# High half first: reordering the three products of each weight unit in a two-block transformer on one Trainium2 core

## What is computed

```python
xn = rms_norm(h, g_mix[l]); proj = xn @ w_in[l]          # four mixers on the parts of proj
h = h + jnp.concatenate([ya, yb, yc, yd], axis=-1) @ w_out[l]
h = h + memory_cross_attention(rms_norm(h, g_xa[l]), rms_norm(mem, g_mem[l]), w_xq[l], w_xkv[l], w_xo[l])
h = h + conv_ffn(rms_norm(h, g_ffn[l]), w_up[l], w_ffconv[l], w_down[l])
...
x = x + gmlp_mixer(rms_norm_2(x, a_norm[l]), a_w_in[l], a_v_norm[l], a_w_sp[l], a_b_sp[l], a_w_out[l])
x = x + diff_attention(rms_norm_2(x, b_norm[j]), k, v, b_w_q[j], b_lambda[j], b_subln[j], b_w_o[j], _lambda_init(l))
x = x + swiglu(rms_norm_2(x, ffn_norm[l]), ffn_w_gu[l], ffn_w_down[l])
return rms_norm_2(x, final_norm)
```

## Time and profile before

| | |
|---|---|
| time of the program, median of 3 runs | 2095.79 us (2094.93 to 2101.04) |
| span of the profiled execution | 2093.4 us |
| the median over that span | 2.4 us |
| PE busy, share of the span | 1982.2 us, 95% |
| DVE, ACT, POOL busy | 51%, 39%, 12% |
| mean granted clock of PE | 0.960 of full speed |

### The profile page before, as it was taken

One profiled execution on the slowest core, in us unless ns is written; L12 is line 12 of the kernel. 1 busy time (PEld: TensorE's weight loads), 2 busy tenths in 40 slices (PEclk: granted clock), 3 DMA queues, 4 the chain that ended last, 5 costly groups with the idle time before them and its releaser, 6 DMA issues.

```text
span 2093.4 us, 25748 instructions
## 1 busy us (share of the span) xinstructions
PE 1982.2 (95%) x8818; PEld 1587.6 (76%) x8818; DVE 1073.7 (51%) x1531; ACT 820.3 (39%) x1216; POOL 256.1 (12%) x206
## 2 busy tenths in 40 slices
PE   6988999889999999899999999999998889999998
PEld 5867776766888878788678888877776568888886
DVE  6666546627777732647444443244676454444323
ACT  4235434415554521453344443134454334444212
POOL 3702102002000000400200000010553020000000
PEclk9988889989999999998999999999997799999999
DMA  4321222112222232221222223222211022232322
GB/s 154 101 91 41 71 72 80 61 45 77 100 90 93 97 110 90 72 93 59 80 94 96 95 95 101 90 83 97 71 51 41 11 71 100 100 100 90 100 90 81
DMA packets 48356, 174.37 MB, mean 83 GB/s; under 512 B 5416, under 2 KB 5544, under 8 KB 48048
## 3 DMA queue, kind: packets, MB, share of 16 engines
q1 hardware_dynamic: 46944, 169.50, 24.1%
q10 hardware_dynamic: 1024, 2.94, 0.4%
q0 software_dynamic: 336, 1.25, 0.2%
HBM read 171.57 MB, written 2.10 MB: 83 GB/s over the span
## 4 chain that ended last, share of the span: by engine, by line
PE 77%; DVE 10%; ACT 5%; issue 5%; POOL 3%; DVEq 0%; ACTq 0%; DMA 0%; POOLq 0%; SPq 0%
PE ps L379 25%; PE ps L380 24%; PE ps L381 24%; POOL square_sum L2028 3%; ACT w_hi L870 2%; DVE w_lo L1367 1%; DVE conv_g L1751 1%; DVE conv_a L1751 1%; PE ps L772 1%; DVE xg_lo L1373 1%; DVE x L1414 1%; DVE r_cols L1380 1%; PE ps L783 1%; PE ps L834 1%; PE ps L532 1%
## 5 line engine op out<-in xcount | busy, mean ns | idle before, releaser
L1367 DVE TENSOR_TENSOR w_lo<-w_raw,w_hi 128x1024 fp32r<-128x1024 f32 x302 | 385.6, 1277 | 593.5 <-ACT w_hi L870 593.4
L379 PE MATMUL ps<-xg_hi,w_hi 128*128 128x512 f32 (+2 forms) x1512 | 593.7, 393 | 43.6 <-DVE xg_lo L1373 18.8
L381 PE MATMUL ps<-xg_hi,w_lo 128*128 128x512 f32 (+2 forms) x1512 | 584.8, 387 | 0.0
L380 PE MATMUL ps<-xg_lo,w_hi 128*128 128x512 f32 (+2 forms) x1512 | 584.7, 387 | 0.0
L870 ACT ACTIVATE w_hi<-w_raw 128x1024 fp32r<-128x1024 f32 x302 | 318.0, 1054 | 678.4 <-PE ps L381 678.4
L379 PEld LDWEIGHTS ps<-xg_hi,w_hi 128*128 128x128 f32 x1512 | 286.0, 189 | 129.4 <-DVE xg_lo L1373 30.5
L381 PEld LDWEIGHTS ps<-xg_hi,w_lo 128*128 128x128 f32 x1512 | 286.2, 189 | 57.7
L380 PEld LDWEIGHTS ps<-xg_lo,w_hi 128*128 128x128 f32 x1512 | 286.4, 189 | 54.0
L379 PE MATMUL ps<-hid_hi,w_hi 128*128 (+1 forms) x528 | 210.2, 398 | 3.5 <-DVE w_lo L1367 3.5
L380 PE MATMUL ps<-hid_lo,w_hi 128*128 (+1 forms) x528 | 209.8, 397 | 0.0
L381 PE MATMUL ps<-hid_hi,w_lo 128*128 (+1 forms) x528 | 209.8, 397 | 0.0
(11 more groups left out here) (319 smaller groups left out, 2586.4 us busy)
## 6 DMA issues: line engine op xcount, KB each, us to landing
w_raw<-in_weights SPq DMA_DIRECT2D x315, 512.0 KB, 3.2
x<-in_x_cols SPq DMA_DIRECT2D x2, 1024.0 KB, 6.9
out_cols<-result SPq DMA_DIRECT2D x8, 256.0 KB, 2.2
squares<-in_mem_cols ACTq DMA_DIRECT2D x1, 512.0 KB, 3.7
sp_w<-in_spatial ACTq DMA_DIRECT2D x1, 512.0 KB, 3.5
sp_b<-in_spatial_bias ACTq DMA_DIRECT2D x1, 512.0 KB, 5.2
dil<-in_dil_table POOLq DMA_DIRECT2D x1, 448.0 KB, 6.6
alibi<-in_alibi_table ACTq DMA_DIRECT2D x1, 448.0 KB
```

Source lines behind the costliest of these rows:

```text
L379: nc.tensor.matmul(to, wh, xh, start=start, stop=False)
L380: nc.tensor.matmul(to, wh, xl, start=False, stop=False)
L381: return nc.tensor.matmul(to, wl, xh, start=False, stop=stop)
L1367: nc.vector.tensor_tensor(w_lo[:, u % 2, :], w_raw[:, u % 2, :], w_hi[:, u % 2, :].bitcast(F32), ALU.subtract).then_inc(w_ready, 1)
```

## The change

In `panel`, `values` and `into_residual` the 16 matmuls of a unit that use `w_hi` are issued first, behind a wait for `w_hi_ready` alone, and the 8 that use `w_lo` come last, behind the wait for `w_ready`. The number, shape and operands of the matmuls stay, and so does everything on the other engines. The functions that run between pieces of attention keep `product`.

```diff
+            def with_hi(to, wh, xh, xl, start):
+
+                nc.tensor.matmul(to, wh, xh, start=start, stop=False)
+                nc.tensor.matmul(to, wh, xl, start=False, stop=False)
+
+            def with_lo(to, wl, xh, stop):
+                return nc.tensor.matmul(to, wl, xh, start=False, stop=stop)
...
             def panel(u, i, to, hi, lo, chunks_ready=None):
 
-                pe.wait_ge(w_ready, at(u + 1, i, 2))
+                pe.wait_ge(w_hi_ready, at(u + 1, i, 2))
                 for k in range(KC):
                     if chunks_ready is not None:
                         pe.wait_ge(xg_ready, chunks_ready + k + 1)
-                    wh, wl = tile(u % 2, k)
-                    mm = product(to, wh, wl, hi[:, k, :], lo[:, k, :], k == 0, k == KC - 1)
+                    with_hi(to, tile(u % 2, k)[0], hi[:, k, :], lo[:, k, :], k == 0)
+                pe.wait_ge(w_ready, at(u + 1, i, 2))
+                for k in range(KC):
+                    mm = with_lo(to, tile(u % 2, k)[1], hi[:, k, :], k == KC - 1)
                 mm.then_inc(used, 1)
...
                 def unit(k, i, first, final):
                     u = u0 + k
-                    pe.wait_ge(w_ready, at(u + 1, i, 2))
+                    pe.wait_ge(w_hi_ready, at(u + 1, i, 2))
                     pe.wait_ge(ready, at(chunk_ready(k), i, 2))
                     kk = at(k, i, 2)
                     for j in range(KC):
                         if first and j in bank_free:
                             pe.wait_ge(*bank_free[j])
-                        wh, wl = tile(u % 2, j)
-                        mm = product(ps[:, (bank0 + j) % 8, :], wh, wl, hi[:, kk, :], lo[:, kk, :], first, final)
+                        with_hi(ps[:, (bank0 + j) % 8, :], tile(u % 2, j)[0], hi[:, kk, :], lo[:, kk, :], first)
+                    pe.wait_ge(w_ready, at(u + 1, i, 2))
+                    for j in range(KC):
+                        mm = with_lo(ps[:, (bank0 + j) % 8, :], tile(u % 2, j)[1], hi[:, kk, :], final)
                         if final and j < KC - 1:
                             mm.then_inc(proj_sums, 1)
                     mm.then_inc(used, 1)
```

More of the change, by code:

```diff
@@ L406, in values @@
             def values(first, u, hi, lo, n_blocks, banks, per_unit):
-                halves = 2 // per_unit
+                pe.wait_ge(w_hi_ready, u + 1)
+                for kk in range(per_unit):
+                    k = (u - first) * per_unit + kk
+                    for b in range(n_blocks):
+                        xh, xl = (t[:, k, b * P:(b + 1) * P] for t in (hi, lo))
+                        wh = w_hi[:, u % 2, kk * S:(kk + 1) * S]
+                        nc.tensor.matmul(ps[:, banks[b], :], xh, wh, start=k == 0, stop=False)
+                        nc.tensor.matmul(ps[:, banks[b], :], xl, wh, start=False, stop=False)
                 pe.wait_ge(w_ready, u + 1)
@@ L412, in values @@
                     for b in range(n_blocks):
[L413 to L417, removed]
+                        mm = with_lo(ps[:, banks[b], :], hi[:, k, b * P:(b + 1) * P],
+                                     w_lo[:, u % 2, kk * S:(kk + 1) * S], k == KC - 1)
                 mm.then_inc(used, 1)
```

## The result

The changed kernel takes 2116.51 us in the median of 5 runs (2110.65 to 2117.1), the kernel before beside it 2101.04 us (2094.93 to 2101.59). The ratio is 1.0066, with a 95% interval of 1.0047 to 1.0085: slower by 14 us of 2101 (10 to 18). The profiled execution has a span of 2114.7 us where that of before had 2093.4, 21.3 us more, and a mean granted clock of 0.945 where that had 0.960.

A forecast was written before the change was run, and what follows sets the result against it. PE, busy for 95% of the span, was taken to bound the kernel. Stage terms summed to +18.8 us, taking the profiled span from 2093.4 to 2112.2; 2.4 for the median gave 2115 us, range 2100 to 2127.

The forecast's parts named there:

- Matmul rate: In all 278 changed units, 6672 matmuls, the new order was taken to cost nothing: zero.
- slow-pass rival: Bank switches in the low pass of residual units cost 0.007 us per matmul, 16 us more: 2131 us; chance 0.08.
- fast rival: Paired matmuls share tiles and their spacing falls from 0.226 us towards 0.213: 2072 us; chance 0.05.
- Last residual unit: At the end of six residual products, DVE's first `x` add starts 1.7 us late, and the chain behind it.
- First panel: In five chunk-fed panels, ten matmuls instead of three follow the last chunk; the sum of squares starts 2.8 us late.
- term without the clock: In chunk-fed first panels, the sum of squares 2.8 us late, of which the late chunks are 1.7.
- term of the clock: In five chunk-fed first panels the clock falls during the waits: +2.0 us each, 10 us in all.
- `w_out`, bank 4: In `w_out`'s first unit PE reaches bank 4 earlier, before DVE frees it, and waits: +1.0 us.
- Loses DVE's 1.28 us, -1.3: At `down`'s third unit, the wait keeps ACT's copy on the path but loses DVE's 1.28 us: -1.3 us.
- Nothing is gained: Inside the loop of `up`, no unit waits longer for `w_lo` than the cited rows show, so no gain.
- End of the kernel: In `down1`, DVE's eight adds end at 2081.7 instead of 2079.0, delaying squares, sums, root and output: +2.7 us.
- Saved waits: At several stages units start earlier without waiting for `w_lo`; all such waits, 16.2 us in 11 pieces, cap the gain.

The follow-up runs named there:

- e1: The changed kernel with one more matmul behind each chunk but the last in the five first panels that wait for chunks: 2104.34 us, 1.0036 of before.
- e2: The changed kernel with the last unit of each product into the residual back in the old order: 2098.48 us, 1.0006 of the kernel before.
- e3: The changed kernel with the five first panels that wait for chunks back in the old order: 2094.37 us, 0.9987 of the kernel before.
- e9: The kernel before with the new order only in the five first panels that wait for chunks: 2117.34 us, 1.0090 of the kernel before.
- e10: The kernel before with the new order only in the last unit of each product into the residual: 2112.79 us, 1.0068 of the kernel before.
- e5: The kernel of e4, but every unit waits for `w_lo` before its first matmul: 2097.78 us, 1.0003 of the kernel before.
- e4: The changed kernel with both the last residual units and the five chunk-fed first panels in the old order: 2081.82 us, 0.9929 of the kernel before.
- e8: The kernel before with the new order only in the `values` units: 2098.06 us, 1.0003 of the kernel before.
- e12: The kernel of e4 with all units of the products into the residual in the old order: 2087.80 us, 0.9954 of the kernel before.
- e6: The kernel of e4 with the first unit of bank-waiting residual products in the old order too: 2083.81 us, 0.9937 of the kernel before.

## Why the prediction was right, point by point

**The result** was forecast at 2115 us, +18.8 in the profile's terms and slower with a chance of 0.83. The median is 2116.5, the spans differ by 21.3, and the ratio asks for 14 us (10 to 18). The mechanism is shown by e1, e2, e3, e9 and e10; the size is a little over what the ratio holds. That 2115 and 2116.5 lie so close is partly luck. The forecast started from a kernel before of 2095.79 us, and the one beside the result took 2101.04; and in the profile the stretches of mixers and attention, for which nothing was forecast, moved by -3.1 and +3.4 us and nearly cancelled.

**Matmul rate, zero.** Right, shown by the windows to the matmul, and by e5. The slow-pass rival (+16) and the fast rival are both out. Why residual products and panels have different spacings stays open; it is not the order, for both orders show the same two numbers.

**Last residual unit, 1.7 us.** The unit started 6.69 us later than before, the first add 8.38: 1.69. The other five show 1.56 to 1.69. With the end of the kernel it makes the 0.0058 to 0.0068 of e3 against e4 and of e10.

**First panel.** The term without the clock was 1.1 beyond the late chunks, e1 shows 1.17 and 1.18, but 1.85 at `w_in`, which was mis-sized. The term of the clock was 2.0 each and 10 in all, the traces show 1.27 to 2.34, and 9.5. The fall was argued from two stretches with less work; it came in all five first panels, and at `up` halfway through, at 495.9. At `gu0` the clock recovered earlier, hence its 1.27. The rule of the Trainium skill (TensorE: Matmul & The Clock Gate, Why this matters for your kernels), which warns of idle gaps between bursts and names longer ones than these, would have left the clock up. Here the longest idle piece between the chunks of `up` was 0.95 us, and the clock was at 0.50 from 495.9 on. So the trace does not agree with it, and the measurement decides.

**The other terms**, from the starts of PE's units in both profiles:

| stage | predicted | measured |
|---|---|---|
| `w_in` | +2.1 | +2.67 |
| mixers, to the start of `w_out` | 0 | +0.1 |
| `w_out`, bank 4 | +1.0 | +0.9 |
| `xq` | +4.4 | +4.2 |
| attention, to the start of `xo` | 0 | -1.7 |
| `xo` and `up` to its third panel | +4.7 | +4.2 |
| loop of `up`, and `down` | -1.3 | -0.8 |
| `a_v` | +0.2 | +0.2 |
| `a_u` | -1.0 | -1.1 |
| mixer, to the second unit of `a_out` | 0 | -1.5 |
| `a_out` and `gu0` | +3.6 | +2.9 |
| `kv_v` | -1.2 | -0.8 |
| `qk` and attention, to the second unit of `bo` | 0 | +3.3 |
| `bo` and `gu1` | +3.6 | +3.9 |
| end | +2.7 | +4.9 |
| sum | +18.8 | +21.4 |

The rows of attention and mixers are the clock. The last of them, before and then with the change, has the same 265 matmuls in 80.5 and 83.7 us, at a granted clock of 0.70 and 0.67:

```profile
1586.27:1666.78 80.51, 68.26 (x265) 43.69 (x263) 41.27 (x96) 35.53 (x83) 11.77 (x9) 0.70 0.04 14
...
1595.73:1679.42 83.69, 71.41 (x265) 45.39 (x264) 41.31 (x96) 35.60 (x83) 11.78 (x9) 0.67 0.04 14
```

In the other two the granted clock is higher with the change, 0.83 to 0.80 and 0.73 to 0.69. e4 and e8 lose 2.8 and 3.1 us in the same stretch as the changed kernel loses 3.3.

Three steps were mistaken or mis-sized.

- *"Loses DVE's 1.28 us, -1.3" at `down`.* The wait stayed (3.64 us). "Nothing is gained" in the loop of `up` was wrong too: windows of the two profiles in that loop, first before and then with the change, show 262 and 267 matmuls in 60 us, both with PE counted as busy throughout.

```profile
580.00:640.00 60.00, 60.00 (x262) 48.37 (x261) 42.08 (x54) 31.56 (x39) 0.00 (x0) 1.00 0.29 97
...
590.00:650.00 60.00, 60.00 (x267) 49.64 (x266) 41.74 (x53) 32.07 (x40) 0.00 (x0) 1.00 0.28 96
```

  There the old loop took 0.2 us longer for each pair of units than a dense one, with no wait in the profile; I read this as short waits that hide in the modelled durations. PE gained 1.1 us there on DVE and ACT, arrived at `down` that much earlier than they did, and paid it back in the wait. One microsecond, gained in another place than I had it.
- *End of the kernel.* DVE's adds ended 2.54 us later against their unit (19.04 against the unit's 16.50), as forecast. But from their end to PE's next step behind the root (L870, before L854) 6.57 us passed where 4.24 had. The 32 small matmuls between, which sum the squares by rows (L863, before L847), took 6.87 us; before they took 2.73 and 1.05. The clock is at 0.50 from 2096.8 on, 0.15 us behind their start; in before it fell only at 2083.3, behind them. In e10, where it falls only at 2097.7, they take 2.20 and 3.20 us, and 1.04 of the 2.33 us is left. I had taken the adds for the whole of the delay.
- *Saved waits.* I counted about 10 us, net of the new wait at `w_out`; the medians of e4 show 15 (11 to 18) and of e12 10 (6 to 13), and by the unit starts both have 10. All the waits for `w_lo` in the trace are 16.2, so 15 would be nearly the cap.

## What to carry to other kernels

Split a wait where PE would really start earlier, and keep the order in which results are handed over: the last unit of a stage should complete its banks one by one, and a unit that is fed chunk by chunk should do all it can with each chunk. Both kinds can be told from the code, and with them left in the old order the same idea went from 1.0066 to 0.9929 of the time. When a change thins out PE's work in a waiting stretch, count what follows at half the clock as well, and not only the work that moved. And a saved wait is worth nothing if the engine that feeds the next hand-over has not become earlier too; follow it to the next point where both meet.

## What the runs showed beyond this

The clock decides more of the time than expected, in places that no edit touched. Runs of the unchanged kernel beside e1 to e4 spread from 2091.48 us at a granted clock of 0.962, over many near 2095 at 0.960, to 2101 at 0.957 and 2104.28 at 0.957. The first attention, from 140 to 292 us, shows how, in windows of e4, whose profiled execution was the slowest of its six, and of e6, whose profiled one was the second fastest of its six:

```profile
140.00:292.00 152.00, 137.69 (x698) 110.19 (x696) 85.57 (x215) 69.46 (x157) 30.94 (x40) 0.78 0.18 61
```

```profile
140.00:292.00 152.00, 137.31 (x740) 110.39 (x739) 88.58 (x218) 73.48 (x163) 30.95 (x40) 0.83 0.19 65
```

Both have PE busy for 137 us, one with 698 and one with 740 matmuls. In e4's profile the first add of `w_out` is 4.20 us late for this, though its first panel was 0.17 early; in e6's it is 3.21 early. What decides which stretch of the attention falls to the lower clock was not settled. It means that an edit worth 3 us can be hidden by the scatter of the attention behind it, as `kv_v`'s gain was in e8, and that single profiles have to be compared stage by stage and not by their spans.
